# Float32r transposes of softmax, values and x in a two-block attention kernel, with a float32 difference added for a quarter of the tokens

## The reference

```python
p = jax.nn.softmax(jnp.where(mask, s + bias, MASK_VALUE), axis=-1)      # block 1, 8 heads
outs.append(jnp.einsum('bhqk,bkhd->bqhd', p.astype(v.dtype), v[:, :q1]))
...
p = e / (jnp.sum(e, axis=-1, keepdims=True) + jnp.exp(sink - m))        # block 2, windowed
p = jax.nn.softmax(s, axis=-1)                                          # block 2, latent
...
x = x + rmsnorm(merged @ w_out[l], post_norm_mix[l])
y = jnp.square(jax.nn.relu(h2 @ w_up[l])) @ w_down[l]
x = x + rmsnorm(y, post_norm_mlp[l])                                    # the result
```

## Time and profile before

| | us |
|---|---|
| median of 3 runs (lowest, highest) | 929.59 (929.24, 929.68) |
| profiled execution: span from first to last instruction | 928.3 |
| PE busy in it | 919.0 |
| DVE busy | 657.3 |
| ACT busy | 483.0 |
| POOL busy | 113.8 |

### The profile page before, as it was taken

The page is one execution under the profiler, slowest core; times in us unless marked ns, Lnnn a source line. Parts: engine busy times, 40 slices in busy tenths (PEclk is TensorE's granted clock), DMA queues, the critical chain, the costliest instruction groups (busy, mean ns, idle before and its releaser), DMA issues.

```text
span 928.3 us, 13427 instructions
## 1 busy us (share of the span) xinstructions
PE 919.0 (99%) x5050; PEld 750.9 (81%) x5050; DVE 657.3 (71%) x1163; ACT 483.0 (52%) x880; POOL 113.8 (12%) x122
## 2 busy tenths in 40 slices
PE   9999999999999999999999999999999999999997
PEld 8778777777898777777777889988888888888886
DVE  7668759888749787766564751879556857775787
ACT  6455346355555355644543324578646435634554
POOL 2003202431040001100000213000000000000015
PEclk9999999999999999999999999999999999999999
DMA  7322112112232411212212355433633453363245
GB/s 252 96 87 68 47 47 80 58 46 80 91 114 88 168 46 55 77 54 78 65 50 69 114 181 182 159 91 90 225 100 95 146 160 100 82 203 115 68 100 151
DMA packets 28048, 97.01 MB, mean 104 GB/s; under 512 B 3280, under 2 KB 4240, under 8 KB 27728
## 3 DMA queue, kind: packets, MB, share of 16 engines
q1 hardware_dynamic: 24864, 85.04, 28.2%
q0 software_dynamic: 2544, 6.62, 3.9%
q10 hardware_dynamic: 576, 4.49, 1.3%
HBM read 85.65 MB, written 4.19 MB: 97 GB/s over the span
## 4 chain that ended last, share of the span: by engine, by line
PE 85%; DVE 9%; ACT 3%; issue 2%; DVEq 0%; ACTq 0%
PE PB L446 13%; PE PB L448 12%; PE PB L447 12%; PE PB L1046 5%; PE PB L1047 5%; PE PB L1048 5%; PE PB L653 4%; PE PB L690 3%; PE PB L668 2%; DVE wl L1559 2%; PE PB L893 2%; PE PB L894 2%; PE PB L895 2%; PE PB L491 2%; PE PB L487 2%
## 5 line engine op out<-in xcount | busy, mean ns | idle before, releaser
L446 PE MATMUL PB<-hh,wh 128*128 128x512 f32 x576 | 234.9, 408 | 0.0
L448 PE MATMUL PB<-hh,wl 128*128 128x512 f32 x576 | 224.7, 390 | 0.0
L447 PE MATMUL PB<-hl,wh 128*128 128x512 f32 x576 | 224.5, 390 | 0.0
L1559 DVE TENSOR_TENSOR wl<-raw,wh 128x1024 fp32r<-128x1024 f32 (+2 forms) x114 | 143.1, 1255 | 70.4 <-ACT wh L1071 70.1
L1071 ACT ACTIVATE wh<-raw 128x1024 fp32r<-128x1024 f32 (+2 forms) x114 | 116.4, 1025 | 71.2 <-PE PB L491 14.0
L446 PEld LDWEIGHTS PB<-hh,wh 128*128 128x128 f32 x576 | 108.1, 188 | 28.1 <-issue 6.2
L448 PEld LDWEIGHTS PB<-hh,wl 128*128 128x128 f32 x576 | 108.1, 188 | 23.3
L447 PEld LDWEIGHTS PB<-hl,wh 128*128 128x128 f32 x576 | 108.3, 188 | 22.7 <-issue 1.9
L1238 ACT ACTIVATE S<-S,sm 128x256 f32<-128x256 f32 (+3 forms) x96 | 50.6, 529 | 105.0 <-DVE sm L1662 80.7
L1071 ACT ACTIVATE wh<-AR 128x1024 fp32r<-128x1024 f32 x56 | 59.0, 1057 | 53.0 <-PE PB L1048 51.0
L1559 DVE TENSOR_TENSOR wl<-AR,wh 128x1024 fp32r<-128x1024 f32 x56 | 68.0, 1221 | 17.6 <-ACT wh L1071 17.4
(11 more groups left out here) (400 smaller groups left out, 1825.6 us busy)
## 6 DMA issues: line engine op xcount, KB each, us to landing
AR<-in_dn SPq DMA_DIRECT2D x40, 512.0 KB, 4.4
raw<-in_upe SPq DMA_DIRECT2D x28, 512.0 KB, 3.5
raw<-in_w2g SPq DMA_DIRECT2D x16, 512.0 KB, 3.4
raw<-in_w1e SPq DMA_DIRECT2D x10, 512.0 KB, 3.4
raw<-in_w1q SPq DMA_DIRECT2D x8, 512.0 KB, 3.5
raw<-in_woab SPq DMA_DIRECT2D x8, 512.0 KB, 3.5
AR<-AR POOLq DMA_DIRECT2D x8, 512.0 KB, 4.5
raw<-in_w2e SPq DMA_DIRECT2D x5, 512.0 KB, 4.3
```

Of the source, the lines that this page charges most:

```text
L446: e.matmul(bank[:], a[:, col(k)], xa[:, k, :], start=k == 0, stop=False)
L447: e.matmul(bank[:], a[:, col(k)], xb[:, k, :], start=False, stop=False)
L448: i = e.matmul(bank[:], b[:, col(k)], xa[:, k, :], start=False, stop=k == 7)
L1559: e.tensor_tensor(wl[c % 3][:, 0:n], raw_of(c), wh[c % 3][:, 0:n].bitcast(F32), ALU.subtract).then_inc(*up("lo", c))
```

## The change

Transposes of S tiles, of the values and of x read the same bytes under a float32r name (`XW` and `SW` are names for the memory of `X` and `S`), write the same PSUM banks under a float32r view, and take as identity `unit`, a float32r copy of `ident` that ACT makes once at the start. No data is rounded on the way: S and X are written as before. For token block 2, x is transposed a second time, in float32, into banks 2 and 3; `final(2, h)` copies that to SBUF, subtracts it from the float32r transpose, forms the result as before, and adds the difference times 2^20. Block 3 of x moves behind the last product.

```diff
@@ turn
-                            i = e.transpose(bank[:, col(m)], soft(n, b)[:, k:k + 128], ident)
+                            i = e.transpose(bank[:, col(m)].bitcast(F32R), SW[:, 2 * (n % 2) + b, k:k + 128], unit[:])
@@ values, t == 1 of block 2
-                        i = e.transpose(values[:, col(m)], S[2][:, col(m)], ident)
+                        i = e.transpose(values[:, col(m)].bitcast(F32R), SW[:, 2, col(m)], unit[:])
@@ turned_x
+                for h in range(2) if b == 2 else ():
+                    bank, before = tenant(2 + h, "fd", h)
+                    e.wait_ge(*to(*before))
+                    for k in range(4):
+                        i = e.transpose(bank[:, col(k)], X[:, 4 * h + k, col(b)], ident)
+                    i.then_inc(*up("xd", h))
...
-                        i = e.transpose(bank[:, col(k)], X[:, 4 * h + k, col(b)], ident)
+                        i = e.transpose(bank[:, col(k)].bitcast(F32R), XW[:, 4 * h + k, col(b)], unit[:])
@@ around the last product
-                        turned_x(3, 2)
...
-                        turned_x(0, 4)
+                        turned_x(3, 4)
+                        turned_x(0, 2)
                         turned_x(1, 6)
@@ act
+            e.activation(unit[:], ident, ACT.Copy).then_inc(*up("tri", 1))
@@ final
+                if b == 2:
+                    e.wait_ge(*to("xd", h))
+                    e.tensor_copy(ar(9216 + 512 * h, 512), seat["fd", h][:]).then_inc(*up("fd", h))
+                    e.wait_ge(*to("fd", h))
+                    e.tensor_tensor(ar(9216 + 512 * h, 512), seat["fin", b, h][:], ar(9216 + 512 * h, 512), ALU.subtract).then_inc(*up("fa0", h))
+                    e.scalar_tensor_tensor(YG[b][:, t], YG[b][:, t], FAC[:, b:b + 1], seat["fin", b, h][:],
+                                           ALU.mult, ALU.add).then_inc(*up("fa1", h))
+                    e.wait_ge(*to("fa1", h))
+                    e.scalar_tensor_tensor(YG[b][:, t], ar(9216 + 512 * h, 512), float(2.0 ** 20), YG[b][:, t],
+                                           ALU.mult, ALU.add).then_inc(*up("fin", b, h))
+                    return
```

More of the change, by code:

```diff
@@ L201, in sb @@
             return ctx.enter_context(nc.sbuf_tensor(name, shape, dt))
+        with nc.sbuf_tensor("XW", [128, 8, T], F32R) as XW:
+            pass
         X = sb("X", [128, 8, T])
@@ L224, in build @@
         sel = sb("sel", [128, 8], F32R)
+        unit = sb("unit", [128, 128], F32R)
         R, acc = sb("R", [128, T]), sb("acc", [128, T])
         with nc.sbuf_tensor("bh", [128, 4, 768], F32R) as bh:
+            pass
+        with nc.sbuf_tensor("SW", [128, 4, T], F32R) as SW:
             pass
```

## The result

| kernel | median us (lowest to highest, runs) | before beside it | ratio to before, 95% interval |
|---|---|---|---|
| the changed kernel | 931.05 (930.49 to 931.91, 18) | 929.68 | 1.0015, 1.0008 to 1.0022 |

The prediction was 925.6, faster. The changed kernel is slower than the one before by 0.15%: within the 0.2% that the prediction counts as no change, with an interval that lies above 1. Its profiled execution has a span of 929.7 us where before has 928.3, so 1.4 us came in.

The account below looks back on a forecast made before the run. PE, busy 99%, bounds the kernel up to the last product, then DVE's last list sets the end. PE saves 8.1 us, DVE loses 4.1: -4.0, from the median 929.59 to 925.6; range 922.9 to 934.2.

Parts of the forecast that it names:

- The load stays short: Transposes on PE: a float32r transpose keeps the float32 transpose's 140-ns load, so the load does not set its step.
- The rival's premise: No faster transposes, chance 0.29: float32r transposes get the 188-ns load, step 0.10 to 0.12; or need two passes.
- Streaming sets 0.067: Transposes on PE: streaming the identity's 128 columns sets a float32r step of 0.067 us, instead of float32's 0.109.
- its own threshold of 0.088: Transpose step in us from which the rival of no faster transposes decides; above it the forecast counts as wrong.
- The reading that I had set aside: Transposes on PE: the block's load, not streaming, bounds the step, at 0.10 to 0.12 us with nothing gained.
- The last transpose keeps its cost: Turns of S: each of 32 calls saves nothing on its last transpose, so 184 transposes save 7.7 us.
- Given back in the attention: Rival, chance 0.06: faster PE comes too early for DVE's and ACT's softmax; half of 7.7 us returns, 929.5.
- Values and x: PE outside the turns of S: values save 0.1 us, x ahead of the last product 0.3 us.
- DVE's last list: Behind the last product: each `final(2, h)` becomes four instructions on the path, 2.70 us for 0.66; 4.1 us lost.
- The covers for blocks 3, 0 and 1 of x: Behind the last product: their transposes stay hidden behind DVE's work; a lost cover costs under 1 us.
- ACT's copy: Start of the kernel: the 128x128 copy for `unit` precedes an idle stretch of 1.06 us and costs nothing.

Follow-up runs that it names:

- the probe: Rows of twelve short transposes or matmuls put between 512-column matmuls, into the changed kernel without second x transposes and with the old end; 935.75 us, one run.
- e5: Changed kernel without second x transposes and with the old end, `weighted` moved directly behind `turn` in all three attention parts; 929.45 us, 0.9995 of the kernel before.

## Why the prediction was wrong, step by step

**The load stays short: right.** 141 ns, by the group of loads. The rival's premise, 188 ns, did not come.

**"Streaming sets 0.067": the step that failed.** I took a 140-ns load for one that bounds nothing, because loads of 137 ns let pairs of 64 columns go by at 0.07. A load's duration is not its step. In the probe 191 ns go with a step of 0.107, 135 ns of a 64-column load with 0.060 or less, and 142 ns of a transpose with 0.083: loads of nearly the same duration go with different steps. Only the first two of a call step by 0.062, near my 0.067. The prediction let the load decide only at 0.10 to 0.12; with 0.086 for most transposes, its own threshold of 0.088 was almost reached. The reading that I had set aside, that the load bounds the step, was right. The Trainium skill (TensorE: Matmul & The Clock Gate, LDWEIGHTS) gives a load as its columns divided by 1.2, in ns, an estimate of 107 for 128. L1016's mean step of 0.107 agrees with it, the transpose's 0.083 does not.

**"The last transpose keeps its cost": half right.** It keeps it, and the matmul behind comes later on top: by 0.06 to 0.07 (once 0.19) at 25 of the 32 calls, where it has 256 or 512 columns, and not at all at the six where it has 64 or 128 (at one it waits). By the ends of all matmuls of both traces up to 510 us, the transposes save 6.4 us, and the matmuls behind the 32 calls give 1.7 back without their waits. So 4.7 in place of 7.7. Counted in the same way the prediction has 216 x 0.042 = 9.1 saved and 32 x 0.042 = 1.3 given back, so of the missing 3.0 some 2.7 are the step and the rest the matmul behind.

**Given back in the attention: a rival with the right mechanism and a small size.** About 1.4 us by those ends, 1.1 by the list of waits; it priced half of 7.7.

**Values and x.** Behind the attention PE is 3.2 us ahead of the kernel before, at `added(3, 6, 0)` 3.3: the x ahead of the last product is worth about 0.1, not 0.3. PE's sum is 3.3 instead of 8.1: of the missing 4.8, 3.0 lie in the turns and 1.4 in the attention's waits.

**DVE's last list: right.** 4.3 in place of 4.1, and 0.17 of it is the one instruction that POOL held up. The covers for blocks 3, 0 and 1 of x held: no instruction of DVE waits for them. Block 1's last eight transposes run at a granted clock of 0.50 behind PE's two waits, and nothing came of that either:

```profile
919.70:921.80 2.10, 0.87 (x8) 0.94 0.00 0
921.80:924.00 2.20, 1.25 (x8) 0.50 0.60 240
```

(PE of the changed kernel by stretches: us, busy and count, granted clock, DMA share, GB/s.)

**ACT's copy: right,** nothing.

**What no term held:** 0.45 us of landing of the last store. Without it the changed kernel would still not have been faster: -3.3 + 4.3 is +1.0.

**The range.** 931.05 lies inside 922.9 to 934.2, but that is luck: the range reached there for transposes at the pace of a 188-ns load or in two passes, and neither came. A step between 0.07 and 0.088 stood in no case of the prediction; with the measured 0.086 its own sum makes 194 x 0.023 = 4.5 us off PE, so -0.4 in all, no change.

## What to carry to other kernels

A load's duration in the trace is not the step that it allows, so for short matmuls a probe of a dozen in a row, with one size changed at a time, says more than any row of another shape. What stands behind the last product is paid in full, and the same instructions are free in the hole ahead of it: look there first, and look which other engine's instructions hold up the one that is to fill the hole. When an order of steps is moved, look at the longest wait that it makes on PE, since one of 2 us cost more than twice its length.

## What the runs showed of the hardware

- A float32r transpose of 128x128 steps by 0.083 us in a row of twelve, a float32 one by 0.108, an ordinary float32r matmul with the same load and stream by 0.107, and one with a 64-column load by 0.060. A 512-column matmul behind float32r transposes ends 0.306 after them instead of 0.23, behind ordinary short float32r matmuls 0.281, behind float32 transposes 0.239.
- Behind a wait of 2.08 us that followed short matmuls, TensorE's granted clock was 0.50 for some 6.8 us (e5). At the end of the changed kernel it was still 1.00 behind a wait of 0.90 us, and 0.50 behind the next one of 1.23 us, with eight transposes between them. Behind one of 1.44 us in block 2 (e5, 370 us) it was 1.00.
- A copy of 64 columns on VectorE took 1.33 us beside a GpSimd instruction of 1.28 and 0.18 without one; an instruction with two inputs in SBUF 1.53 instead of 0.68.
- Six more instructions on VectorE brought one more 8-KB packet of the instruction queue behind the last store.
